# A two-block hybrid transformer on one core: stationary router weights, the first gather ahead of the branch, a shorter addition behind the last expert, and features evicted ahead of their rounding

## The reference

```
for layer m in the first block (m = 0..3):
    shift, scale, gate = silu(c) @ ada_w[m] + ada_b[m]
    h = x * (1 + scale) + shift
    y = mixer(h)  or  swiglu(h)  or, at m = 3, moe(h)
    x = layer_norm(ALPHA * x + (1 + gate) * y) * g + b

moe(h):
    logits = h @ w_router                       # 256 x 8
    top_v, top_i = top_k(logits, 2)
    combine = one_hot(top_i) weighted by softmax(top_v)   # 256 x 8
    y = sum over e of combine[:, e] * ((silu(h @ w1[e]) * (h @ w3[e])) @ w2[e])

second block (m = 4..7): h = rms_norm(x) * g * (1 + scale) + shift;  x = x + gate * y
```

## Time and profile before

| | |
|---|---|
| runs, median (lowest to highest) | 2206.36 us (2204.56 to 2209.4) |
| the profiled execution: time, span | 2206.33 us, 2204.5 us |
| PE matmuls busy | 2007.6 us, 91% of the span |
| PE weight loads | 1737.4 us, 79% |
| DVE busy | 1692.5 us, 77% |
| ACT busy | 1166.0 us, 53% |
| mean granted clock of PE | 0.945 of 2.4 GHz |
| moved from memory | 551.40 MB read, 251 GB/s over the span |

### The profile page before, as it was taken

How to read it: one execution, slowest core, us unless ns; L and a number is a source line. 1 busy time by engine, 2 the same in 40 slices (tenths; PEclk the granted TensorE clock), 3 DMA queues, 4 the chain that set the end, 5 groups by cost and what they waited for, 6 DMA issues and landing times.

```text
span 2204.5 us, 28342 instructions
## 1 busy us (share of the span) xinstructions
PE 2007.6 (91%) x11552; PEld 1737.4 (79%) x11552; DVE 1692.5 (77%) x1776; ACT 1166.0 (53%) x1270; POOL 73.1 (3%) x121
## 2 busy tenths in 40 slices
PE   6878899878889999999999999868779999969999
PEld 6666899777668887878788788767669998858998
DVE  6675888876578989898898988888778896675444
ACT  3543434364257777777677766544543345544332
POOL 6001000000000000000000000000010000000000
PEclk9988999988799999999999999979889999988999
DMA  9743699732369999999999999926229995323552
GB/s 352 232 163 134 252 340 372 277 128 96 134 222 332 352 361 365 333 347 376 344 337 361 367 331 354 329 93 214 96 77 329 354 369 170 115 76 104 184 191 96
DMA packets 251209, 554.37 MB, mean 251 GB/s; under 512 B 10076, under 2 KB 75856, under 8 KB 251072
## 3 DMA queue, kind: packets, MB, share of 16 engines
q1 hardware_dynamic: 247252, 544.13, 69.3%
q0 software_dynamic: 3552, 8.29, 1.1%
q10 hardware_dynamic: 268, 0.07, 0.0%
HBM read 551.40 MB, written 1.05 MB: 251 GB/s over the span
## 4 chain that ended last, share of the span: by engine, by line
PE 70%; DVE 15%; ACT 7%; issue 4%; DMA 4%; SPq 0%; DVEq 0%; ACTq 0%
PE bank L489 21%; PE bank L490 21%; PE bank L491 21%; DVE ring_lo L1897 4%; ACT ring_hi L1240 2%; PE bank L878 1%; DMA ring<-in_w_in_dram 1%; DVE acc L1837 1%; DMA ring<-in_ffn_w_dram 1%; PE bank L571 1%; PE bank L1064 1%; DMA ring<-in_ada_w_dram 1%; DVE work L2080 1%; ACT work L1366 1%; PE bank L540 1%
## 5 line engine op out<-in xcount | busy, mean ns | idle before, releaser
L1897 DVE TENSOR_TENSOR ring_lo<-ring,ring_hi 128x2048 fp32r<-128x2048 f32 x417 | 950.2, 2286 | 253.0 <-ACT ring_hi L1240 250.1
L1240 ACT ACTIVATE ring_hi<-ring 128x2048 fp32r<-128x2048 f32 x417 | 795.2, 1913 | 477.3 <-PE bank L491 228.0
L489 PE MATMUL bank<-hh,ring_hi 128*128 128x256 f32 x1152 | 333.5, 289 | 25.0 <-DVE ring_lo L1897 10.3
L490 PE MATMUL bank<-hl,ring_hi 128*128 128x256 f32 x1152 | 330.8, 287 | 0.0
L491 PE MATMUL bank<-hh,ring_lo 128*128 128x256 f32 x1152 | 330.5, 287 | 0.0
L489 PE MATMUL bank<-ring_hi,hh 128*128 128x256 f32 (+2 forms) x672 | 222.1, 331 | 37.4 <-DVE hl L1961 12.0
L489 PEld LDWEIGHTS bank<-hh,ring_hi 128*128 128x128 f32 x1152 | 226.4, 196 | 29.8 <-issue 13.1
L491 PE MATMUL bank<-ring_hi,hl 128*128 128x256 f32 (+2 forms) x768 | 244.8, 319 | 0.0
L489 PE MATMUL bank<-ring_hi,hgh 128*128 128x512 f32 (+1 forms) x576 | 220.4, 383 | 7.9 <-DVE ring_lo L1897 3.1
L490 PEld LDWEIGHTS bank<-hl,ring_hi 128*128 128x128 f32 x1152 | 226.5, 197 | 0.7 <-issue 0.2
L491 PEld LDWEIGHTS bank<-hh,ring_lo 128*128 128x128 f32 x1152 | 226.1, 196 | 0.0
(11 more groups left out here) (409 smaller groups left out, 2813.4 us busy)
## 6 DMA issues: line engine op xcount, KB each, us to landing
ring<-in_moe_w_dram SPq DMA_DIRECT2D x264, 1024.0 KB, 5.3
ring<-in_ada_w_dram SPq DMA_DIRECT2D x48, 1024.0 KB, 7.4
ring<-in_w_mod_dram SPq DMA_DIRECT2D x48, 1024.0 KB, 7.3
ring<-in_w_in_dram SPq DMA_DIRECT2D x40, 1024.0 KB, 5.9
ring<-in_ffn_w_dram SPq DMA_DIRECT2D x33, 1024.0 KB, 5.5
ring<-in_w_gate_dram SPq DMA_DIRECT2D x22, 1024.0 KB, 5.0
ring<-in_w_up_dram SPq DMA_DIRECT2D x22, 1024.0 KB, 5.0
ring<-in_w_down_dram SPq DMA_DIRECT2D x22, 1024.0 KB, 5.1
```

Source lines behind the costliest of these rows:

```text
L489: pe.matmul(ps, xh, wh, start=first, stop=False)
L490: pe.matmul(ps, xh, wl, start=False, stop=False)
L1240: act.activation(ring_hi[i % NH][:, 0:z], ring[n % NS][:, 0:z], ACT.Copy).then_inc(*s.hi(("hi", home(s, i), i)))
L1897: dve.tensor_tensor(ring_lo[n % NS][:, 0:z], ring[n % NS][:, 0:z], hi, ALU.subtract).then_inc(*s.lo(("lo", home(s, i), i)))
```

## The change

It does five things. (1) In `modulated`, for all m, DVE evicts the pairs 0 and 2 first and then makes all low halves; ACT evicts pair 1, rounds 0 and 1, evicts 3, rounds 2 and 3. (2) The router's weights are stationary (8 columns) and 256 token columns move; the logits come out as 8 rows, are copied by DVE, turned by PE in two small transposes, and copied again. PE's gate sum is made ahead of the counting. (3) DVE makes the first one-hot tiles right behind the positions, and `gather_first` and `first_rows` with its halves run before the branch. The row update of tile 0 goes into group 1, `xl` into group 2, and one `low_halves` behind the router. (4) In expert 7's groups 4 and 5 DVE makes YK = YK * gate + ALPHA * X (`weighed`); the last scattered results are then multiplied by `comb` and the gate in one operation and added, inside the branch, and only the statistics follow. In `moe_all` the residual moves into the branch. (5) The warm-up square root on ACT signals and waits for its predecessor.

```diff
@@ tensor_program
             def router():
                 ps = psum("router")
+                pe.wait_ge(*at("router weights"))
+                for kc in range(8):
+                    if kc % 2 == 0:
+                        pe.wait_ge(*at("h", 3, kc // 2))
+                    x = product(ps[0:8, 0:256], rth[:, kc, :], rtl[:, kc, :], hh[:, kc, :], hl[:, kc, :], kc == 0, kc == 7)
+                x.then_inc(*main.small(("router",)))
+                ps = psum("router turned")
+                pe.wait_ge(*at("router rows made"))
                 for t in range(2):
-                    for kc in range(8):
-                        z = slice(128 * t, 128 * t + 128)
...
-                        x = product(ps[:, 8 * t:8 * t + 8], hh[:, kc, z], hl[:, kc, z], rth[:, kc, :], rtl[:, kc, :], kc == 0, kc == 7)
-                x.then_inc(*main.small(("router",)))
+                    x = pe.transpose(ps[:, 8 * t:8 * t + 8], lgT[:, 128 * t:128 * t + 128], ident[0:8, 0:8])
+                x.then_inc(*main.turn(("router turned",)))
+                summed((3, "router"))
                 ps = psum("places")
...
             router()
-            summed((3, "router"))
+            gather_first(0)
+            gather_first(1)
             pe.wait_ge(*at("flag"))
@@ scalar_program
             def modulated(m):
+                for odd in (1, 3):
+                    act.wait_ge(*at("h", m, "turned", odd))
+                    if odd == 1:
+                        act.wait_ge(*at("cols", m, 1))
+                    ps = R.of("h", m, odd)
+                    for i in range(2):
+                        kc = 2 * odd + i
+                        x = act.activation(hT[:, kc, :], ps[:, 256 * i:256 * i + 256], ACT.Identity, bias=cols[:, m, kc:kc + 1], scale=cols[:, m, 8 + kc:9 + kc])
+                        x.then_inc(*main.act(("hT", m, kc), ("free", "h", m, odd)))
+                    for kk in (odd - 1, odd):
                         act.wait_ge(*at("hT", m, 2 * kk + 1))
+                        act.activation(hh[:, 2 * kk:2 * kk + 2, :], hT[:, 2 * kk:2 * kk + 2, :], ACT.Copy).then_inc(*main.act(("hh", m, kk)))
...
             high_halves(main, moe0 + EARLY - 1)
+            summed((3, "router"))
             act.wait_ge(*at("router margins"))
             act.activation(rv2, rv2, ACT.Exp).then_inc(*main.act(("router exp",)))
-            summed((3, "router"))
+            first_rows()
             act.wait_ge(*at("flag"))
@@ vector_program
             def modulated(m):
+                for kk in (0, 2):
...
+                        x = dve.tensor_scalar(hT[:, kc, :], ps[:, 256 * i:256 * i + 256], cols[:, m, 8 + kc:9 + kc], cols[:, m, kc:kc + 1], ALU.mult, ALU.add)
+                        x.then_inc(*vec(("hT", m, kc), ("free", "h", m, kk)))
                 for kk in range(4):
...
                     z = slice(2 * kk, 2 * kk + 2)
                     dve.wait_ge(*at("hh", m, kk))
                     dve.tensor_tensor(hl[:, z, :], hT[:, z, :], hh[:, z, :].bitcast(F32), ALU.subtract).then_inc(*vec(("h", m, kk)))
...
                 dve.wait_ge(*at("router"))
-                dve.tensor_copy(lg, R.of("router")[:, 0:16].rearrange("p (t c) -> p t c", t=2)).then_inc(*vec(("free", "router")))
+                dve.tensor_copy(lgT, R.of("router")[0:8, 0:256]).then_inc(*vec(("router rows made",), ("free", "router")))
+                dve.wait_ge(*at("router turned"))
+                dve.tensor_copy(lg, R.of("router turned")[:, 0:16].rearrange("p (t c) -> p t c", t=2)).then_inc(*vec(("free", "router turned")))
...
                 dve.tensor_tensor(rv2, rv2, rv1, ALU.subtract).then_inc(*vec(("router margins",)))
+                settled()
+                for t in range(2):
+                    x = dve.tensor_scalar(ga_S[:, 0, t, 1, :], iota, posm[:, t, 0:1], None, ALU.is_equal)
+                x.then_inc(*vec(("few", "S", 0)))
...
                     if G == 1:
+                        layer_rows(3, YK, (0,), few)
+                    if e == 7 and g in (4, 5):
+                        weighed(g - 4)
+                    if G == 2:
                         dve.wait_ge(*at("few", "xh"))
                         dve.wait_ge(*at("few", "gathered", 0, 1))
                         dve.tensor_tensor(xl[:, :, :], XN[:, :, :], xh.bitcast(F32), ALU.subtract).then_inc(*s.vec(("few", "xl")))
...
+                def weighed(t):
+
+                    for h in range(2):
+                        c = slice(512 * h, 512 * h + 512)
+                        dve.wait_ge(*at("gate", 3, h))
+                        dve.wait_ge(*at("free", "scatter", 6, t, h))
+                        dve.tensor_tensor(YK[:, t, c], YK[:, t, c], gate[0][:, c], ALU.mult).then_inc(*s.vec())
+                        dve.wait_ge(*s.vec.last())
+                        dve.scalar_tensor_tensor(YK[:, t, c], X[:, t, c], ALPHA, YK[:, t, c], ALU.mult, ALU.add).then_inc(*s.vec())
...
-                        if e == 0:
+                        if e == 7:
+                            dve.scalar_tensor_tensor(XN[:, t, c], ps[:, :], comb[:, t, e:e + 1], gate[0][:, c], ALU.mult, ALU.mult).then_inc(*s.vec())
+                            dve.wait_ge(*s.vec.last())
+                            x = dve.tensor_tensor(XN[:, t, c], XN[:, t, c], YK[:, t, c], ALU.add)
...
             modulated(3)
-            layer_rows(3, YK, (0,))
-            low_halves(main, moe0 + EARLY - 1)
             router()
             summed((3, "router"))
+            low_halves(main, moe0 + EARLY - 1)
+            first_rows()
             settled()
...
-            boundary(3, lambda t, h: YK[:, t, 512 * h:512 * h + 512], lambda t, h: [("drained", e) for e in range(3)])
+            dve.drain().then_inc(*s_drain[2](("drained", 2), *(("r", 3, t, h) for t in range(2) for h in range(2))))
+            for e in range(3):
+                dve.wait_ge(*at("drained", e))
+            for t in range(2):
+                for h in range(2):
+                    statistics(4, t, h, XN, ("r", 3, t, h))
+                spread(4, t)
+            for t in range(2):
+                normalized(4, t, XN)
             layer_rows(4, YTr)
```

More of the change, by code:

```diff
@@ L1017, in router, with gather_first @@
                 x.then_inc(*main.small(("places",)))
+            def gather_first(half):
+                ps = psum("gather", 0, half)
+                if half == 0:
+                    pe.wait_ge(*at("few", "S", 0))
+                for k in range(4):
+                    kc = 4 * half + k
+                    for t in range(2):
+                        x = pe.matmul(ps[:, 128 * k:128 * k + 128], XN[:, t, 128 * kc:128 * kc + 128], ga_F[:, 0, t, 1, :], start=t == 0, stop=t == 1)
+                x.then_inc(*main.small(("few", "gathered", 0, half)))
             def moe_all():
@@ L1024, in moe_picked @@
                 s = few
-                def gather_first(half):
-                    ps = psum("gather", 0, half)
-                    if half == 0:
-                        pe.wait_ge(*at("few", "S", 0))
-                    for k in range(4):
-                        kc = 4 * half + k
-                        for t in range(2):
-                            x = pe.matmul(ps[:, 128 * k:128 * k + 128], XN[:, t, 128 * kc:128 * kc + 128], ga_F[:, 0, t, 1, :], start=t == 0, stop=t == 1)
-                    x.then_inc(*s.small(("few", "gathered", 0, half)))
                 def gather(p, q):
@@ L1224, in scalar_program @@
         def scalar_program(act):
-            done = [0]
+            done, roots = [0], {}
             def high_halves(s, upto):
@@ L1258, in roots_next @@
             def roots_next():
-                act.activation(warm[:, :], ones[:, 0:1], ACT.Sqrt)
+                if "roots" in roots:
+                    act.wait_ge(*roots["roots"])
+                act.activation(warm[:, :], ones[:, 0:1], ACT.Sqrt).then_inc(*main.act())
+                roots["roots"] = main.act.last()
             def together(m):
@@ L1635, in mixer2, with first_rows @@
                     high_halves(main, ahead(turn_of["wout2", l, i]))
+            def first_rows():
+                act.wait_ge(*at("few", "gathered", 0, 0))
+                for k in range(4):
+                    x = act.activation(hg[0][:, k, :], R.of("gather", 0, 0)[:, 128 * k:128 * k + 128], ACT.Identity, bias=cols[:, 3, k:k + 1], scale=cols[:, 3, 8 + k:9 + k])
+                x.then_inc(*main.act(("free", "gather", 0, 0)))
+                act.wait_ge(*main.act.last())
+                for half in range(2):
+                    if half:
+                        act.wait_ge(*at("few", "hg", 0, 3))
+                    z = slice(4 * half, 4 * half + 4)
+                    act.activation(hgh[0][:, z, :], hg[0][:, z, :], ACT.Copy).then_inc(*main.act(("few", "hgh", 0, half)))
             def moe_all():
@@ L1924, in normalized, with layer_rows @@
                 dve.tensor_scalar(XN[:, t, :], src[:, t, :], mv[:, t, 0:1], mv[:, t, 1:2], ALU.subtract, ALU.mult).then_inc(*vec(("xn", i, t)))
```

(16 more changed lines are left out.)

71 lines of the change are left out of this document (17 added, 54 removed).

## The result

The changed kernel takes 2179.06 us (median of 4 runs, 2176.38 to 2183.34); the kernel before took 2205.46 beside it. The ratio is 0.9879 [0.9857, 0.99]. Run again in another session it took 2178.21, ratio 0.9866 [0.9848, 0.9884]. The forecast was 2186, with 2175 to 2199 as its range: right in sign and within the range, but the gain was 26.4 us where 20.6 were summed, and 2179 lies outside the 2181 to 2191 that I gave the forecast itself. The two profiled spans differ by more, 29.9 us (2204.5 and 2174.6); the profiled execution after was the fastest of its four.

The account below looks back on a forecast made before the run. PE bounds the experts; between stages a chain through DVE and ACT does, with PE half idle. 12.0 + 9.3 - 4.1 + 3.4 = 20.6, so 2206.3 - 20.6 = 2185.7, say 2186 us; range 2175 to 2199.

Parts of the forecast that it names:

- swallowed: Stage starts: low clock and weight tiles leave PE 6 us or less of 12; 2194 us, chance 0.16.
- (b): Stage starts: PE's denser starts avoid the low clock, up to 2 us more per stage; 2177 us, chance 0.12.
- Part 1: Features of the stages, evictions ahead of halves: DVE and ACT 2.4 us earlier; gain 12.0 us (6.8 to 16).
- At that clock PE ends block 3 at 8.0 instead of 9.2, so 1.2 is left: Mixer starts (m = 0, 2, 4, 6): at low clock PE keeps 1.2 of 2.4 us; taken 1.8, 1.8, 1.9, 1.7.
- its stall of 1.31: m = 5: PE's stall at the second weight tile; less 0.3, a gain of 1.0 us.
- Part 2: m = 3 features to experts: shorter router, gather ahead of the branch; gain 9.3 us (6 to 12).
- Rival (c): Branch behind the early gather: DVE and ACT fetch in turn, PE waits idle; 2191 us, chance 0.15.
- Part 3: Experts: work added to DVE stalls PE, two `weighed` blocks at 1.5 us each included; loss 4.1 us (1.5 to 6.5).
- xl and the row update 1.1: Experts: row update in place of xl in group 1 costs 0.2 us, xl in group 2 costs 0.9.
- The gemv of the modulation: Experts: nearest rows for DVE's added work, 2.60 us in one place; PE stalled 0.58, 1.17 and 1.02.
- Part 4: End of the experts: DVE's chain to the row update 11.3 us instead of 14.7; gain 3.4 (2.8 to 3.6).
- (d): Branch: PE, idle for 3.6 us, falls to 1.2 GHz into the experts; 2216 us at 60 us, chance 0.02.

Follow-up runs that it names:

- the others' means: Mean stage lengths over the study's other traces: two with the old features, five with the new, set against each other.
- the two filled kernels: Changed kernel, and it without the new features, each with unread matmuls ahead of m = 4 and among the sums: 2187.46 us (new features), 2205.37 (old).
- the filled pieces: Changed kernel with the unread filling matmuls and VectorE's added work in smaller pieces (`weighed` in four places, xl in two halves): 2181.35 us, ratio 0.9891.

## Why the prediction was right, and what it mis-sized

**The parts gave time where they were said to.** None of the four took the other sign, and the rivals of a change that is swallowed, taken back at the branch or lost to the clock did not come. The rival that came, in part, is (b): the low stretch of the clock ended earlier as well. It had a chance of 0.12 against the 0.50 of the forecast as summed.

**Part 1 is the term that was mis-sized: 12.0 against 16 to 21.** Its schedule of DVE and ACT held, a little better than worked out (4.93 to 5.24 for 5.4). What failed is the step "At that clock PE ends block 3 at 8.0 instead of 9.2, so 1.2 is left": it carried a shift through at a fixed clock, and left an earlier end of the low clock to rival (b). Shown: at m = 6 the lead grows from 0.8 to 2.5 us over 24 matmuls without a wait, by matmuls at full rate where before they ran at half; at m = 1 the same behind the stall. By the 12th microsecond of m = 2, 4 and 6 PE is 2.7, 2.7 and 2.5 us ahead of the kernel before, nearly the whole lead of DVE and ACT (2.7 to 3.0), where some 1.8 was put down. The median, 2179, lies nearer to (b)'s 2177 than to 2186.

By stage, m = 2, 4 and 6 gave 3.5 to 3.8 in the others' means, twice their terms and above the 2.5 that I had set as their upper bound, and m = 1 gave 4.0 for 3.0. m = 0 gave 1.1 for 1.8. m = 7 was right.

m = 5 was wrong: its stall of 1.31 is gone from the trace after, and the stage is no shorter. PE's idle time there fell by 1.1 us (3.5 to 2.4), while the work it lost by low clock (its busy time by one less the granted clock, over windows of 1 us) rose by 1.8. The kernel before, run again, explains it: there the low clock lasts to 8.9 us into m = 5 (5.6 in the first trace, 8.5 after), the stall isn't in the trace at all, and the stage is 200.2 long. So the stall belonged to one execution, in which PE had its clock back early and then waited for the weights; there was no 1.0 to gain. Why the low stretch differs between executions the traces don't show.

What is argued and not shown is how the whole of 3.5 to 3.8 splits in the mixers: 2.5 are seen within 9 us of the start at m = 6, the rest comes in the chain behind, and keeping the clock up by other work gave 0.5 us at m = 4. There a difference in low clock isn't even needed: in the two filled kernels with the new and the old features the clock is low for 3.4 us of m = 4 alike once its products run, and the stages still differ by 3.7, with PE 3.1 ahead by the 12th microsecond. So at m = 4 it may be that the lead of DVE and ACT simply arrives whole, without the discount that I made for the low clock.

**Part 2, 9.3 against 9.2,** is right in sum by luck, twice over. Two errors cancel: the gather ran at a granted clock of 0.5 to 0.6 for most of it and ended 1.3 later than put (5.84 for 5.18, and a start 0.6 late), and the branch cost ACT 2.74, not 4.0. Both were in the bounds. And the 46.6 it is measured from is one execution's: in before again the gather takes 6.25 instead of 5.18 and the first expert products run at half clock, so that the gain would be 11.8, near the upper bound of 12. The Trainium skill ("Advanced Engine Details and Errata", Control Flow Timing) gives a compare-and-branch about 108 ns. The idle time at the branch, which holds the load of the count into a register too, was 2.74 us on ACT here and 4.02 on DVE before, so the trace doesn't agree with that figure as the price of this branch. Rival (c) fell: the early gather keeps 6.1 us at the stall.

**Part 3, -4.1 against -3.7,** and its terms: `weighed` 3.0 (2.8 when it is taken out, with stalls of 1.28 and 1.09), xl and the row update 1.1 (0.8 are left without `weighed`: 791.4 to 792.2). The three new stalls stand where they were put, one in group 2 and one in each of the last two groups. The gemv of the modulation was a good stand-in for both.

**Part 4, 3.4 against 3.3.** The chain of 11.3 came out to the tenth, with some luck: the terms listed for its last piece add up to 5.3 (2.6 + 0.8 + 1.9), not the 5.1 that the sum uses. Against what it puts into the experts it leaves 0.5, about the 0.4 that my own terms gave (3.4 - 3.0); so this edit, taken by itself, moved nothing that can be measured, and I could have said so.

**(d)** PE's wait at the branch was 2.28, and the experts ran at 1.00 as before.

## What to carry to other kernels

Where the matmul engine starts a stage at low clock, earlier features needn't be discounted for it: 2.6 to 2.9 us on VectorE and ScalarE gave 3.5 to 4.0 by the end of the stages m = 1, 2, 4 and 6, where 1.7 to 3.0 were put down. Cost the shift at the clock of before, and then again with the low stretch ending earlier. The reverse doesn't hold: extra work that only kept the clock up brought 0.5 us at m = 4, where the chain of VectorE and ScalarE sets the pace. And trace the kernel before twice: the stall of 1.31 us at m = 5 stood in one of two executions, and m = 3 differed by 2.6 us. Work moved into a stretch bound by TensorE costs a third to a half of its length in stalls when it comes in one piece of 2 to 3 us (0.8 to 1.3), and much less in pieces of half the size (0.9 in all for what had cost 3.2); set it against what it saves before moving it.

## What the runs showed of the hardware

The granted clock fell while TensorE was busy without a pause. Windows of 1 us ahead of m = 2 in the changed kernel (run again), where 32 matmuls of one column run from 424.58 to 428.41 and transposes follow at once:

```profile
426.00:427.00 1.00, 1.00 (x11) 1.00 (x11) 0.97 (x2) 0.00 (x0) 0.00 (x0) 1.00 1.03 418
427.00:428.00 1.00, 1.00 (x10) 1.00 (x11) 0.66 (x4) 0.20 (x1) 0.00 (x0) 0.92 1.00 391
428.00:429.00 1.00, 1.00 (x6) 1.00 (x7) 0.96 (x3) 0.18 (x1) 0.42 (x1) 0.50 1.08 385
```

PE is busy for the whole microsecond in each row, and yet the clock goes to 1.2 GHz. A busy share of 1.00 is no promise of the full clock. But it doesn't fall each time, and wide matmuls between the narrow ones don't prevent it. The transposes of m = 2 in the changed kernel, in the same kernel run again, in the filled one and in the filled pieces:

```profile
426.54 1.94 PE L573 MATMUL bank<-cst,XN 128*128 128x128 f32 x16
428.28 3.39 PE L573 MATMUL bank<-cst,XN 128*128 128x128 f32 x16
429.39 1.94 PE L575 MATMUL bank<-cst,XN 128*128 128x128 f32 x16
430.86 3.65 PE L575 MATMUL bank<-cst,XN 128*128 128x128 f32 x16
```

They take 1.94 us at the full clock, and both pairs have it once. Each trace has six such places (m = 1, 2, 3, 5, 6 and 7). Without filled sums (ten traces) all the transposes are at the full clock in 11 of 60; with them (three traces) in 4 of 18. The first half of the transposes, which follows the sums without a pause, is slowed (1.3 us or more instead of 1.07) in 14 of 60 without the filling and in 14 of 18 with it. So the eight wide matmuls did not keep the clock up here; if anything it fell sooner. What does decide it the traces don't show.
